# A triangular inverse kept as four 32x32 blocks instead of two 64x64 blocks

## The reference, cut to what matters

```python
def step(s, inp):
    r_t, w_t, k_t, v_t, kk_t, a_t = inp
    s_kk = jnp.einsum('bhvk,bhk->bhv', s, kk_t)
    s = (s * w_t[:, :, None, :]
         - s_kk[..., None] * (kk_t * a_t)[:, :, None, :]
         + v_t[..., None] * k_t[:, :, None, :])
    return s, jnp.einsum('bhvk,bhk->bhv', s, r_t)
```

## Time and profile before

| what | value |
| --- | --- |
| time, median of 3 runs | 5635.92 us (5633.05 to 5637.43) |
| the profiled execution's own time | 5637.04 us |
| its span in the profile | 5635.4 us |
| TensorE busy, share of the span | 4840.7 us, 86% |
| VectorE busy | 3900.1 us, 69% |
| ScalarE busy | 1440.5 us, 26% |
| recurrence stage, layer 1 and layer 2 | some 332 us each, from 684 and from 3493 us |

### The profile page before, as it was taken

The page is one execution under the profiler, slowest core; times in us unless marked ns, Lnnn a source line. Parts: engine busy times, 40 slices in busy tenths (PEclk is TensorE's granted clock), DMA queues, the critical chain, the costliest instruction groups (busy, mean ns, idle before and its releaser), DMA issues. The chain is left out here.

```text
span 5635.4 us, 77264 instructions
## 1 busy us (share of the span) xinstructions
PE 4840.7 (86%) x29492; PEld 2635.4 (47%) x29492; DVE 3900.1 (69%) x8899; ACT 1440.5 (26%) x3642; POOL 1550.1 (28%) x1408
## 2 busy tenths in 40 slices
PE   8988899978898888888789888998888988888787
PEld 4545588643343334333345455885433434343332
DVE  4556677558787777777644566775677877777776
ACT  1122311312222232322210332213122222222222
POOL 0100000024444444444300000000244444444443
PEclk9999899989999999999999998999999999999999
DMA  3223610669999999999932235106799999999999
GB/s 144 73 77 113 242 57 33 233 267 427 417 421 425 410 427 419 426 412 420 395 127 71 77 138 217 57 33 237 288 427 415 418 427 408 427 415 427 416 422 391
DMA packets 306839, 1644.76 MB, mean 292 GB/s; under 512 B 34697, under 2 KB 48265, under 8 KB 140833
## 3 DMA queue, kind: packets, MB, share of 16 engines
q0 software_dynamic: 193504, 1370.70, 58.4%
q1 hardware_dynamic: 112960, 269.08, 12.9%
HBM read 1575.84 MB, written 63.82 MB: 291 GB/s over the span
## 5 line engine op out<-in xcount | busy, mean ns | idle before, releaser
L2224 PE MATMUL psum<-peer_rows,peer_diagonal 128*128 128x512 f32 x5120 | 2503.4, 623 | 516.1 <-ACT peer_diagonal L2286 513.9
L2157 POOL DMA_INDIRECT peer_rows<-in_peer_rows,look_up_index x1280 | 1480.9, 1157 | 2814.7 <-PE psum L2224 1632.8
L2367 DVE CUSTOM_DVE_ANT_0 peer_rows<-peer_rows,h_rows 128x1024 f32<-128x1024 f32 x1280 | 1552.8, 1226 | 482.1 <-DMA peer_rows<-in_peer_rows,look_up_index 468.2
L2224 PEld LDWEIGHTS psum<-peer_rows,peer_diagonal 128*128 128x128 f32 x5120 | 934.0, 197 | 1546.4 <-issue 833.6
L2280 ACT ACTIVATE peer_active<-peer_dots 128x2 f32<-128x2 f32 (+1 forms) x642 | 130.7, 204 | 2021.4 <-DVE peer_dots L2367 2021.2
L2286 ACT ACTIVATE peer_diagonal<-ident_sb,peer_weight 128x128 f32<-128x128 f32 x1280 | 444.2, 394 | 145.8 <-DVE peer_weight L2320 144.7
L2171 PEld LDWEIGHTS psum<-h_sb,query_weights 128*128 128x128 f32 x1184 | 234.4, 198 | 302.3 <-issue 302.3
L473 PE MATMUL psum<-in_weights,h_sb 128*128 128x512 f32 (+1 forms) x800 | 309.9, 549 | 0.0
L2320 DVE TENSOR_TENSOR peer_weight<-peer_active,peer_share 128x2 f32<-128x2 f32 (+1 forms) x642 | 104.0, 162 | 201.1 <-ACT peer_active L2280 201.1
L1008 PE MATMUL psum<-h_sb,rw_in_gate_weights 128*128 128x512 f32 (+1 forms) x768 | 213.7, 439 | 29.3 <-DMA rw_in_gate_weights<-in_w_gate 29.3
L2171 PE MATMUL psum<-h_sb,query_weights 128*128 128x128 f32 x1184 | 234.2, 280 | 0.0
(11 more groups left out here) (378 smaller groups left out, 5708.7 us busy)
## 6 DMA issues: line engine op xcount, KB each, us to landing
rw_out_mod_weights<-in_w_mod SPq DMA_DIRECT2D x16, 2048.0 KB
in_weights<-in_w_in SPq DMA_DIRECT2D x12, 2048.0 KB, 9.3
peer_rows<-in_peer_rows,look_up_index POOLq DMA_INDIRECT x1280
scratch_rw_scratch<-rw_in_direction SPq DMA_DIRECT2D x20, 768.0 KB, 6.3
wkv_own<-scratch_rw_scratch SPq DMA_DIRECT2D x20, 768.0 KB, 5.6
rw_in_gate_weights<-in_w_gate POOLq DMA_DIRECT2D x24, 512.0 KB, 5.9
scratch_rw_scratch<-rw_in_z SPq DMA_DIRECT2D x10, 1024.0 KB, 5.7
wkv_r_kk<-scratch_rw_scratch SPq DMA_DIRECT2D x40, 256.0 KB, 6.4
```

What stands on the lines that cost most here:

```text
L2157: nc.gpsimd.indirect_dma_start(rows[spot][:, :], None, t.dram["peer_rows"], bass.IndirectOffsetOnAxis(ap=index[j % 4][:, k:k + 1], axis=0) ...
L2224: last = nc.tensor.matmul(t.bank[2 * (i % 2) + c], diagonal[k % DIAGONALS][:, :], rows[spot][:, D + c * 512:D + (c + 1) * 512], start=(j = ...
L2367: v.tensor_tensor_reduce(rows[spot][:, 0:D], rows[spot][:, 0:D], h[:, :], 1.0, 0.0, ALU.mult, ALU.add, dots[b][:, k:k + 1]).then_inc(s["do ...
```

## The change

The inverse is kept as the four 32x32 blocks on T's diagonal (`QUARTERS`), for levels 1 to 4. Each level's inner product of a direction is then 4 heads x 4 blocks = 16 products of 32x32, its outer products 32; they sit on the four diagonal 32x32 tiles of the array. All of VectorE's work on them has half the columns (masks 128x128, adds 128x256), `begin_turned_inverse` has 4 instructions of 32x128 for a direction in place of 2 of 64x256, and `side_of` 16 products in place of 8.

The fifth level, which joins two 32-blocks to a 64-block, is done only for the off-diagonal 32x32 block: 8 inner products from the early to the late rows, a plain copy (no mask), 8 outer products, and VectorE copies the result (two copies of 32x128 for a direction) into a new full 64x64 tile `full_turned`. The diagonal blocks of that tile are copied there by ScalarE (`spread_turned`, four copies for a direction, once the fourth level is added). `solve_first` and `solve_second` read `full_turned`, and `solve_first` waits for `spread` as well.

```diff
@@ side_of, and inner of levels 1 to 4
-                    for rows in BLOCKS:
-                        last = mm(pass_bank(d, 1)[rows, h * HB:(h + 1) * HB], gram[d][n % 2][rows, h, 0, rows], t.ident[rows, rows], start=True, stop=True)
+                    for rows in QUARTERS:
+                        last = mm(pass_bank(d, 1)[rows, h * QB:(h + 1) * QB], gram[d][n % 2][rows, h, 0, rows], t.ident[rows, rows], start=True, stop=True)
...
@@ solve_first
                     wait("added", d, LEVELS * (n + 1))
+                    wait("spread", d, n + 1)
                     wait("rhs_copied", d, n + 1)
...
-                        last = mm(pass_bank(d, 0)[rows, h * HD:(h + 1) * HD], inverse[n % 2][d][rows, 1, h, :], rhs[d][rows, h, :], start=True, stop=True)
+                        last = mm(pass_bank(d, 0)[rows, h * HD:(h + 1) * HD], full_turned[d][rows, h, :], rhs[d][rows, h, :], start=True, stop=True)
...
@@ TensorE, level b
+                            if b < LEVELS:
+                                for rows in QUARTERS:
+                                    last = mm(banks(d)[0][rows, h * QB:(h + 1) * QB], gram[d][n % 2][rows, h, 0, rows], inverse[n % 2][d][rows, 0, h, :],
+                                              start=True, stop=True)
+                            else:
+                                for early, late in zip(EARLY[d], LATE[d]):
+                                    last = mm(banks(d)[0][late, h * QB:(h + 1) * QB], gram[d][n % 2][early, h, 0, late], inverse[n % 2][d][early, 0, h, :],
+                                              start=True, stop=True)
...
+                                for rows in QUARTERS:
+                                    mm(banks(d)[1][rows, h * QB:(h + 1) * QB], inverse[n % 2][d][rows, 1, h, :], inner[d][rows, h, :], start=True, stop=True)
+                                for rows in QUARTERS:
+                                    last = mm(banks(d)[1][rows, (4 + h) * QB:(5 + h) * QB], inner[d][rows, h, :], inverse[n % 2][d][rows, 1, h, :],
+                                              start=True, stop=True)
+                            else:
+                                for early, late in zip(EARLY[d], LATE[d]):
+                                    last = mm(banks(d)[1][early, h * QB:(h + 1) * QB], inner[d][late, h, :], inverse[n % 2][d][late, 1, h, :], start=True, stop=True)
...
@@ ScalarE
+            def spread_turned(n, d):
+                wait("zeroed_turned", d, 1)
+                wait("added", d, LEVELS * n + LEVELS - 1)
+                for j, rows in enumerate(QUARTERS):
+                    last = nc.scalar.copy(full_turned[d][rows, :, j % 2 * QB:(j % 2 + 1) * QB], inverse[n % 2][d][rows, 1, :, :])
+                last.then_inc(signal("spread", d), 1)
...
+                for d in range(2):
+                    spread_turned(n, d)
                 if n % 2 == 0 and n + 2 < STEPS:
                     for d in range(2):
                         exponentials(n // 2 + 1, d)
...
@@ VectorE, level b
+                        else:
+                            v.tensor_copy(inner[d][:, :, :], blocks(banks(d)[0][:, 0:4 * QB])).then_inc(signal("inner_masked", d), 1)
...
+                        else:
+                            for early in EARLY[d]:
+                                last = v.tensor_copy(full_turned[d][early, :, (1 - d) * QB:(2 - d) * QB], blocks(banks(d)[1][early, 0:4 * QB]))
+                            last.then_inc(signal("added", d), 1)
```

More of the change, by code:

```diff
@@ L1144, in wkv_stage @@
     HB = P // 2
+    QB = P // 4
     BLOCKS = (slice(0, HB), slice(HB, P))
+    QUARTERS = [slice(j * QB, (j + 1) * QB) for j in range(4)]
     FIRST, SECOND = (BLOCKS[0], BLOCKS[1]), (BLOCKS[1], BLOCKS[0])
+    EARLY, LATE = (QUARTERS[0::2], QUARTERS[1::2]), (QUARTERS[1::2], QUARTERS[0::2])
     with ExitStack() as mem:
@@ L1154, in wkv_stage @@
         masks = both("masks", 3, P)
-        block_masks = both("block_masks", 7, HB)
+        block_masks = both("block_masks", 6, QB)
         halves = sbuf("halves", 4)
@@ L1162, in wkv_stage @@
         state, first_state, start = both("state", PAIRS, HD), both("first_state", PAIRS, HD), both("start", PAIRS, P)
-        inverse = [both(f"inverse{b}", 2, 4, HB) for b in range(2)]
+        inverse, full_turned = [both(f"inverse{b}", 2, 4, QB) for b in range(2)], both("full_turned", 4, HB)
         rhs, u = both("rhs", 4, HD), both("u", 4, HD)
@@ L1175, in wkv_stage @@
                 [four_grams(unwritten[:, 0:size]), sbuf("gram", 4, 4, P)]]
-        inner = both("inner", 4, HB)
+        inner = both("inner", 4, QB)
         block = mem.enter_context(nc.Block())
@@ L1195, in blocks @@
         def blocks(ap):
-            return ap.rearrange("p (h n) -> p h n", n=HB)
+            return ap.rearrange("p (h n) -> p h n", n=QB)
         @block.sync
@@ L1433, in _ @@
                         for h in range(4):
-                            for rows in BLOCKS:
-                                last = mm(banks(d)[0][rows, h * HB:(h + 1) * HB], gram[d][n % 2][rows, h, 0, rows], inverse[n % 2][d][rows, 0, h, :],
-                                          start=True, stop=True)
+                            if b < LEVELS:
[6 more added lines that the diff above has]
+                                              start=True, stop=True)
                         last.then_inc(signal("inner", d), 1)
@@ L1529, in _ @@
                 v.memset(start[d][:, :, :], 0.0).then_inc(s["zeroed"], 1)
+                v.memset(full_turned[d][:, :, :], 0.0).then_inc(signal("zeroed_turned", d), 1)
             dve.wait_ge(s["zeroed"], 2)
+            for d in range(2):
+                wait("zeroed_turned", d, 1)
             def less_own(i, d):
@@ L2506, in block_constants @@
 def block_constants():
-    i = np.arange(P // 2)
+    i = np.arange(P // 4)
     row, col = i[:, None], i[None, :]
-    out = np.zeros((2, P, 7, P // 2), np.float32)
+    out = np.zeros((2, P, 6, P // 4), np.float32)
     for direction in range(2):
-        for level in range(6):
+        for level in range(5):
             b = 1 << level
             lo_hi = (row // (2 * b) == col // (2 * b)) & (row // b % 2 == 0) & (col // b % 2 == 1)
-            out[direction, :, level] = np.tile(lo_hi if direction == 0 else lo_hi.T, (2, 1))
-        out[direction, :, 6] = np.tile(row == col, (2, 1))
+            out[direction, :, level] = np.tile(lo_hi if direction == 0 else lo_hi.T, (4, 1))
+        out[direction, :, 5] = np.tile(row == col, (4, 1))
     return out
```

30 lines of the change are left out of this document (13 added, 17 removed).

## The result

The changed kernel takes 5726.5 us (median of 4 runs, 5721.0 to 5729.5), the kernel before beside it 5635.4 (4 runs, 5633.1 to 5637.4): a ratio of 1.0161, 95% interval 1.0143 to 1.0178. That is 91 us slower, where I forecast 62 faster, and far outside my range. The profiled execution took 5729.5 us, its span is 5727.6.

A forecast was written before the change was run, and what follows sets the result against it. TensorE's products bound three of the recurrence step's five stretches, the solve's chain and VectorE the others. Both layers -70 and clock +8 made -62 from 5637.0: 5575 us, range 5540 to 5632.

The forecast's parts named there:

- What a product costs: Inner and outer products, levels 1 to 4: array columns set the pace; a round falls from 58.5 to 32 ns.
- stretch by stretch: One recurrence step in five stretches: -0.8, -1.27, 0, -1.0 us, then the boundary at -0.3 or -0.6; layer -35.2.
- my two signs of being wrong: In the profile after: a pitch over 0.1 us, or new TensorE waits at `solve_first` for `spread`.
- TensorE's busy time: Sign in a layer's recurrence stage: TensorE's busy time down by some 60 us.
- The round of four tiles at 32 ns: Inner and outer products: four 32x32 tiles run at once, 26 + 6 = 32 ns a round.
- my second case: Inner and outer products: a 32-column product holds its tile like a 64-column one, round 58.5 ns; +53, 5628 us; chance 0.15.
- The third case: Inner and outer products, levels 1 to 4: four tiles don't run together, a round takes 117 ns; about 5750 us; chance 0.13.
- The clock: At short boundaries TensorE idles more: four or five more clock falls a layer, 0.8 us each, +8 us.
- my -35: One layer's recurrence stage: all stretches and boundaries summed to -35.2 us, before the clock's cost.
- The boundary: From the fourth level's outer products to the next step's first ones, set by VectorE's list: -0.3 us short, -0.6 long.
- ScalarE's eight copies: `spread_turned` copies after level 4: 0.25 us each, 2.0 us a step, nothing on the path; 40 us if uncovered.
- The switches: Tile shape changes around `solve_first`, `cross` and `solve_second`, six a step: 0.12 us each, taken as roughly 0.1.

The follow-up runs named there:

- the kernel with few stops: The changed kernel with the turned inverse's outer products of levels 1 to 4 issued in the first step only: 5620.1 us, ratio 0.9973.
- stream e: In the kernel before, a stream put ahead of TensorE's stage work: 64 times four 32x32 and two 64x64 products; the stream took 42 us.

## Why the prediction was wrong, step by step

**The step that failed** stands in "What a product costs": *"twice as long, so the array's columns and not the issuing of instructions set the pace."* From there on the forecast has no term for the supply of instructions. The sentence is true at half clock, and no proof that a shorter round can be fed at full clock. A round of two 64x64 records is 58.5 ns for four instructions; a block of 256 in 3.73 us is 14.6 ns an instruction, 58.3 ns for four; in 3.45 us it is 13.5 and 54. At full clock both limits stood close together, and the half-clock row could show only the one of them that doubles. What the six nanoseconds are that "don't scale with the clock", no run here shows. The new round asks for 16 instructions in 64 ns (two rounds of four tiles): 4 ns each, for a supply of 13.5 to 14.6.

The term "stretch by stretch" built on it. For columns one to three of the table I had -0.8, -1.27 and -1.0 a step, and they came as +0.3, +2.1 and +1.4. That is 6.9 us a step between forecast and result. In the kernel without the turned outer products the columns are -0.5, -0.1 and -0.6; without the 1.5 us of rounds that it leaves out in them it would be +0.3, so some 3.5 of the 6.9 went with the instructions (an estimate). That kernel still has 1.7 us a step of stops, and a clock of 0.81; how the rest divides between them is open.

Neither of my two signs of being wrong came: the pitch is 0.06 us, and `solve_first` doesn't wait for `spread`. Both ask about the array and ScalarE, none about the supply. TensorE's busy time, forecast 60 us lower in a stage, fell by 5 and 8.

What would have shown it before: the page counts instructions by queue, and 58 blocks in 332 us are 5.7 us each. Twice the inner, outer and side products makes the 91 that came; the densest interval between two packets of the kernel before, about 3.5 us, times 91 is near 320 us, with no slack for the stretches that wait for VectorE.

The Trainium skill, Runtime: NRT & Kernel Launch, Instruction fetch mechanics, says that instructions come in blocks of 16 KB, 256 of them, that the next page is fetched while the current one runs, and that a crossing is mostly hidden. The size of the block agrees with this trace (stops at one index modulo 256, 16 KB a packet); "mostly hidden" does not hold here: 92 crossings of the 180 in the two stages cost 112 us together.

**The round of four tiles at 32 ns** was right (0.06 us for eight records). The Trainium skill, TensorEngine Tiling (Array Packing), Instruction Overhead, gives any matmul some 60 cycles of overhead; I had made my second case of it, a record of 32 columns held as long as one of 64. The runs don't show that: rounds of 32 columns come every 32 ns, those of 64 every 58.5. The third case, "no four together", forecast some 5750, close to the result, but by another mechanism; its number is no merit. In one half sentence it had the right one ("instructions must come at four for what is now two"), which I did not price.

**The clock**, +8 us for four or five more falls a layer: mis-sized. Half clock in a stage went from 17 to 142 and 133 us. What it costs in the changed kernel is open; in the kernel with the fifth level alone 55 us less of it in layer 1 and 58 in layer 2 gave 19 us in all, 0.17 us for each, even with the fillers' time against it. At that rate the 120 us more would be some 20 us a layer (an estimate), so over half of my -35 could have gone even with instructions enough.

**The boundary**, -0.3 a short step: no gain. In the kernel with few stops the short boundary (median of columns four and five) is 6.32 + 4.02 = 10.34 us for 10.31 before, and that kernel leaves out 0.5 us of level 4's outer products in it; in the changed kernel it is 6.95 + 3.97 = 10.92, with stops. The pieces were as I had them (mask of a 128-column tile 0.29 us, addition 0.42, copies and masks of 32 partitions 0.30 each), but no time came back there.

**ScalarE's eight copies** off the path, at 0.30 and not 0.25 us: right. **The switches**, 0.12 us from one row: 0.13 at full clock, 0.17 at half.

## What to carry to other kernels

Count TensorE's instructions beside its columns: an fp32 product is four of them whatever its size, and here they came at 13.5 to 14.6 ns each in most steady stretches. Before cutting products into smaller ones, compare blocks of 256 times 3.5 to 3.7 us with the stretch's time, above all in stretches in which TensorE is busy from end to end; stops that have no releaser and stand at one index modulo 256 are the mark of it. And a row at half clock tells which limit doubles, not which other limit stands close to it at full clock.

## What was new of the hardware

- A block of 256 instructions arrives every 3.45 to 4.0 us in steady streams, fp32 or bf16, up to 6 beside other transfers; about two blocks are in store after a wait (237 fp32 records, 474 instructions, before the first stop; 261 bf16 records, 522). TensorE goes into a new block 1.2 us after the end of its packet at the earliest.
- 14 blocks more in a stage cost 3 us, 33 to 37 more cost some 50: the store hid the shortage at a mean of 4.6 us a block, and no longer at 4.1 to 4.2.
- The loss from the supply does not need the clock: 0.98 of full with 60.7 us of stops in the kernel with split products, 0.81 with 54.3 us in the changed one.
- Changing between 32x32 and 64x64 tiles back and forth costs 0.13 us each way at full clock and 0.17 at half (the mean of both ways, from stream e).
